# Two groups of buffers at the top of SBUF start 32 columns higher

## The reference

```python
# block 1
y = jnp.concatenate([attn, hg, fn], axis=-1) @ w_out[l]
x_new = x + g1 * y
gate, up = jnp.split(h @ w_gu, 2, axis=-1)        # h = modulate(x_new, ...)
x_new = x_new + g2 * ((jax.nn.silu(gate) * up) @ w_dn)
# block 2
x = x + jnp.concatenate([out_a, out_b, out_m], axis=-1) @ w_out[l]
u = h @ w_up                                      # h = rms_norm_2(x, ...)
uc = conv_b + sum(conv_w[i] * up_pad[:, i:i + s] for i in range(CONV_WIDTH))
gate, val = jnp.split(uc, 2, axis=-1)
x = x + (jax.nn.silu(gate) * val) @ w_down
```

```python
sa = jnp.einsum('bhvk,bhk->bhv', state, a_t)
state = (state * d_t[:, :, None, :] + sa[..., None] * b_t[:, :, None, :]
         + v_t[..., None] * k_t[:, :, None, :])
```

## Time and profile before

| what | value |
|---|---|
| median of three runs | 3351.14 us |
| the profiled execution's own time | 3344.78 us |
| its span, first to last instruction | 3343.0 us |
| mean granted TensorE clock | 0.984 |
| TensorE busy | 3163.2 us, 95% |
| VectorE busy | 1454.5 us, 44% |
| ScalarE busy | 1054.2 us, 32% |
| GpSimd busy | 372.4 us, 11% |

### The profile page before, as it was taken

The page is one execution under the profiler, slowest core; times in us unless marked ns, Lnnn a source line. Parts: engine busy times, 40 slices in busy tenths (PEclk is TensorE's granted clock), DMA queues, the critical chain, the costliest instruction groups (busy, mean ns, idle before and its releaser), DMA issues.

```text
span 3343.0 us, 42666 instructions
## 1 busy us (share of the span) xinstructions
PE 3163.2 (95%) x18680; PEld 2433.8 (73%) x18680; DVE 1454.5 (44%) x2104; ACT 1054.2 (32%) x1616; POOL 372.4 (11%) x390
## 2 busy tenths in 40 slices
PE   6999999999899999999998988988889999999999
PEld 2456766666667888888887766777767888888887
DVE  6256634666444311113336444266753444344333
ACT  4243322444333211112213655334433322222211
POOL 1012202334212000000002100011111100000000
PEclk9999999999999999999999999999999999999999
DMA  6011110000023111111212200000012111110212
GB/s 245 32 63 64 63 67 22 17 13 16 10 76 142 48 51 51 51 51 51 76 45 89 85 16 36 19 6 2 3 63 106 60 42 47 51 51 32 101 46 74
DMA packets 35209, 182.33 MB, mean 55 GB/s; under 512 B 4261, under 2 KB 4261, under 8 KB 21584
## 3 DMA queue, kind: packets, MB, share of 16 engines
q1 hardware_dynamic: 22176, 133.18, 11.3%
q0 software_dynamic: 12848, 46.43, 3.6%
HBM read 161.63 MB, written 17.96 MB: 54 GB/s over the span
## 4 chain that ended last, share of the span: by engine, by line
PE 84%; DVE 9%; ACT 4%; DMA 1%; issue 1%; POOL 1%; DVEq 0%; POOLq 0%; ACTq 0%; SPq 0%
PE ps L548 17%; PE ps L550 17%; PE ps L549 17%; PE ps L538 10%; PE ps L687 4%; PE ps L751 3%; PE ps L592 2%; PE ps L1228 2%; DMA ar<-in_xT 1%; PE ps L651 1%; PE ps L1089 1%; PE ps L834 1%; PE ps L609 1%; DVE ar L2089 1%; DVE ar L2095 1%
## 5 line engine op out<-in xcount | busy, mean ns | idle before, releaser
L548 PE MATMUL ps<-r,r 128*128 128x512 f32 x2632 | 1035.1, 393 | 10.7 <-DVE r L2085 5.4
L549 PE MATMUL ps<-r,r 128*128 128x512 f32 x2632 | 1026.4, 390 | 0.0
L550 PE MATMUL ps<-r,r 128*128 128x512 f32 x2632 | 1026.3, 390 | 0.0
L548 PEld LDWEIGHTS ps<-r,r 128*128 128x128 f32 x2632 | 495.4, 188 | 125.4 <-issue 16.2
L549 PEld LDWEIGHTS ps<-r,r 128*128 128x128 f32 x2632 | 495.5, 188 | 104.6 <-issue 3.0
L550 PEld LDWEIGHTS ps<-r,r 128*128 128x128 f32 x2632 | 495.2, 188 | 103.6
L2078 DVE TENSOR_TENSOR r<-ar,r 128x1024 fp32r<-128x1024 f32 (+1 forms) x170 | 204.3, 1202 | 325.1 <-ACT r L1411 325.0
L1411 ACT ACTIVATE r<-ar 128x1024 fp32r<-128x1024 f32 (+1 forms) x170 | 174.4, 1033 | 535.3 <-PE ps L550 495.4
L1449 ACT ACTIVATE ar<-ps 128x256 f32<-128x256 f32 (+3 forms) x330 | 146.9, 470 | 534.6 <-PE ps L538 115.7
L538 PE MATMUL ps<-ar 128*128 128x128 f32 (+4 forms) x1460 | 245.7, 340 | 6.4 <-ACT ar L1449 3.3
L538 PEld LDWEIGHTS ps<-ar 128*128 128x128 f32 (+1 forms) x1460 | 190.8, 186 | 57.4 <-issue 31.8
(11 more groups left out here) (295 smaller groups left out, 3485.6 us busy)
## 6 DMA issues: line engine op xcount, KB each, us to landing
ar<-in_w_mod SPq DMA_DIRECT2D x24, 1024.0 KB, 4.9
ar<-in_w_gu SPq DMA_DIRECT2D x22, 1024.0 KB, 4.8
ar<-in_w_up SPq DMA_DIRECT2D x22, 1024.0 KB, 4.8
ar<-in_w_in SPq DMA_DIRECT2D x19, 1024.0 KB, 4.8
ar<-in_w_dn SPq DMA_DIRECT2D x32, 512.0 KB, 3.5
x<-ar POOLq DMA_DIRECT2D x48, 256.0 KB, 2.3
ar<-x POOLq DMA_DIRECT2D x24, 512.0 KB, 8.1
ar<-in_xT POOLq DMA_DIRECT2D x16, 512.0 KB, 13.8
```

The lines of the kernel that those rows point to most:

```text
L548: M.matmul(o, whk, hi[k][:, a:a + n], start=k == 0, stop=False)
L549: M.matmul(o, whk, lo_[k][:, a:a + n], start=False, stop=False)
L550: ins = M.matmul(o, wlk, hi[k][:, a:a + n], start=False, stop=k == nk - 1)
```

## The change

The name `TAIL` goes, and each place that used it counts from the arena's end instead. `TAIL` was `COLS - 4128` = 49056; `COLS - 4096` is 49088. Both homes (`wh`, `wl`) and the tail tiles of the recurrence start 32 columns, 128 bytes in each partition, higher. Three other uses are ends of regions or an assertion, and no column comes from them. No instruction, wait or transfer is added, removed or moved in any queue. Line numbers after the change are lower by one.

```diff
-TAIL = COLS - 4128
...
-    wh = rounded(TAIL, 2)
-    wl = rounded(TAIL + 2048, 2)
+    wh = rounded(COLS - 4096, 2)
+    wl = rounded(COLS - 2048, 2)
...
-    r5 = Region(FT + 8192, TAIL)
+    r5 = Region(FT + 8192, COLS - 4096)
...
-    r5 = Region(stage_at, TAIL)
+    r5 = Region(stage_at, COLS - 4096)
...
-    assert r9.at <= TAIL
+    assert r9.at <= COLS - 4096
     r8 = Region(ring_at, ring_at + SLOT * NSLOT)
     halves = [[r8.tile(512) for _ in range(6)] for _ in range(2)]
-    r8 = Region(TAIL)
+    r8 = Region(COLS - 4096)
     temps = [[x[:, 0:256] for x in halves[j]] + [r8.tile(256)] for j in range(2)]
     toks = [[r8.tile(512) for _ in range(3)] for _ in range(2)]
```

## The result

The changed kernel took 3388.2 us (median of 4 runs, 3383.55 to 3391.39) against 3350.52 us before (median of 4, 3344.78 to 3351.72). The ratio is 1.0114, with a 95% interval of 1.0100 to 1.0129: it is 38 us slower, where no change was forecast and the range ended at 3362 us. No instruction moved; lines are lower by one.

What follows compares the result with a forecast made beforehand. TensorE was taken as the bound, 3163 of 3343.0 us busy. All terms were 0 against the profiled 3344.78 us; centring near the three runs' median of 3351.14 us gave 3350 us, range 3338 to 3362 us.

Steps and rivals of the forecast that it cites:

- What bounds the kernel: Whole program: TensorE busy 3163 of 3343.0 us; dot3's matmuls start 226.8 ns apart, 13.5 ns beyond their columns.
- What touches moved columns: Split weights: 147 of 170 splits write the tail, so 6936 of 7968 float32r matmuls load weights from moved columns.
- Does the position of the weights count at all: dot3, activation area against tail: both 143 matmuls in 32 us, so distance costs nothing; low address part untested.
- The low part, from the nearest rows: dot3 weight starts against moving operand: float32 rows L609 and L1089 show no cost; term 0, bounds -81 and +194 us.
- The weight load: Loads beside dot3's matmuls: busy 188 ns, idle 38 ns, so up to 38 ns of slower load stays hidden; term 0.
- ACT and DVE, the recurrence: Split writes at L1411 and L2078, and the recurrence's small matmuls and copies: slowdowns hidden or at most 0.5 us; terms 0.
- The second: In dot3, next weights' load beside the running matmul: 11.7 ns more per matmul, 81 us added, 3431 us; chance 0.06.
- The first: In dot3, equal remainders of weights and moving operand cost the 13.5 ns: 81 us less, 3269 us; chance 0.05.
- The Trainium skill's gap of 215.8 ns: Warm dot3 matmuls: if the shift brought this gap instead of 226.8 ns, an estimated 76 us less.
- The third: Surrounding code: a chance stall shifts the sum a few us either way, 3340 to 3360 us; chance 0.05 beyond 6.7 us.
- the rule on 16-byte lines: SBUF reads of dot3 weights: each line crossing costs, but a 128-byte move crosses as many lines, so sum stays 0.

Runs made afterwards that it cites:

- the series: Six kernels with the split weights' homes at twelve distances lower, two per kernel, against the kernel before; 3367.41 to 3394.01 us, one run each.
- kernels with the old relation: Whole arena 128 bytes higher against the kernel before, ratio 0.9988; changed kernel with everything from mix0 to the activation area 32 columns higher, 1.0004.

## Why the prediction was wrong, point by point

**What bounds the kernel.** Right. PE has no idle time in the stretches, so a few ns on each of its matmuls come out whole in the end.

**What touches moved columns.** Right, and it gives the size: 6936 x 5.6 ns = 39 us, where the medians differ by 38 us. The profiled executions have 34.1 us of it between the first and the last `dot3` matmul. Most of the rest is in the window scores between them, which the change does not touch: from 1950.0 us before and from 1974.3 us after, the same 80 passes took 4.3 us less in the changed kernel's execution, at a granted clock of 0.95 against 0.89 (before, then after):

```profile
1950.00:2025.00 75.00, 61.65 (x327) 0.89 0.08 29
L1089 PE MATMUL ps<-ar x80: 376/376/794, 1950.0 to 2024.7; 64*128 64x256 f32 x80
```

```profile
1974.00:2045.00 71.00, 57.13 (x328) 0.95 0.09 30
L1088 PE MATMUL ps<-ar x80: 376/376/636, 1974.3 to 2044.7; 64*128 64x256 f32 x80
```

**Does the position of the weights count at all.** Right as far as it went. Thousands of columns cost nothing, and all tiles moved together cost nothing. As I wrote, that comparison left the low part untested.

**"The low part, from the nearest rows".** This is the step that failed. It put 0 for the new relation, where the runs show 5.6 ns a matmul and 38 us in all, because a float32 row had that relation without a loss (L609) and another had the old one (L1089). Both are float32, two passes and two cycles for each column. The kernel with the moving operand moved turns L609's relation from 32 into 0, and the row stays as in the earlier trace rows (L610 there, first and last start 27.0 us apart):

```profile
L610 PE MATMUL ps<-ar x64: 592/592/593, 143.8 to 170.8; 128*128 128x512 f32 x64
```

So the float32 matmul shows no effect of the relation between 0 and 32, and its rows could not speak for float32r, for or against. I named the weakness ("Float32r reads twice as fast and has no such row") and then took the value of the nearest row anyway. Where every row of a form shares one alignment by construction, the trace holds no evidence on another alignment; the price should then have stayed open between its bounds, -81 and +194 us, instead of 0 with 84% of the chance.

**The weight load.** The load stayed at 188 ns in the changed kernel, as forecast, and its 38 ns of cover were not used. The cover was beside the point: what lengthened is the matmul, which has none.

**ACT and DVE, the recurrence.** Right: L2077 is at 1225 ns, and the tiles of the recurrence alone have the ratio 0.9995.

**The rivals.** The second, "the new relation costs more", was the one that happened, with its sign and its mark in the profile (fewer than 143 in the tail stretch alone). Its cause, the load of the next weights beside the running matmul, was not shown. It had 0.06, for the same faulty reason. Its size was put at 11.7 ns a matmul and measured 5.6. The first was wrong: no place in the series is below 226.8 ns, so the 13.5 ns beyond the columns are not what the old relation costs against any place tried. The Trainium skill's gap of 215.8 ns for 512 columns ("TensorE: Matmul & The Clock Gate", section "Back-to-back issue gap"), which the page gives for a single matmul by itself, was reached by no `dot3` stretch here; the least is 226.6 ns. The third stayed within a few us, as the 0.9988 and 1.0004 of kernels with the old relation show.

**The skill's rules.** From the rule on 16-byte lines ("SBUF — State Buffer", section "Door 1: The DMA port swizzle") I had concluded that a move by 128 bytes cannot matter. The count of lines is the same before and after the move, and the time is not, so the count alone does not give the time. In the series, one line off (4 columns) costs nothing, half a line (2 columns) 6.6 ns and two lines (8 columns) 6.6 ns as well. The same page says, in section "SBUF: two separate sides", that on the engine side only one shared pair of ports causes contention and that PE never waits on anyone. If that is meant of PE's own two reads as well, weights and moving operand, the runs differ: their relation adds up to 7.5 ns to 226.8. No run shows whether a port is what is waited for.

**What stays open.** Shown: at a distance of 32 columns it is the relation of the weight tile to the moving operand that costs, and neither the place of the weights, nor the ring, nor the tiles of the recurrence. Shown for one pair: 64 columns (256 bytes) are as good as 0. Argued only: that both are read at once from the same part of SBUF and one holds up the other. The load beside a matmul can't be all of it, as L550 is long beside an unmoved load. Why 16 columns lower costs a third of its neighbours, why the three lines differ at 24 lower, and why high homes alone cost more than high and low together, was not settled.

## What to carry to other kernels

Where TensorE is the bound and the operands are float32r, place the weight tiles and the moving tiles at starts that agree modulo 256 bytes (one run stood exactly 256 bytes off), and keep that when an arena is laid out anew: a cleanup of 32 columns cost 1.1% here. Other shapes than 128x128 by 128x512 were not tried. When a change moves addresses alone, compare stretches that have moved and unmoved tiles on the same engine; if every tile of a kind shares one alignment, count the effect of another as unknown, and do not borrow a row of another data type.

## What the runs showed of the hardware that was not expected

A float32r matmul of 128x128 by 128x512 starts every 226.8 ns at best in this kernel, and every 229.0 to 234.3 ns at nine other distances between weights and moving operand, while 16 bytes lower and 240 bytes lower cost nothing. One moved load in three makes two matmuls of three long. Passes of a plain float32 matmul of this size take 592 ns at relation 0 and at 32 alike. Moving both operands 128 bytes from the start of SBUF has no effect (0.9988).
